# Grouped-query attention: two context tiles of a head pair as one unit of two banks

## What is computed

```python
def mixer_a(u, uc, q_g, k_g, ang, need_ctx):      # 16 query heads of 64, 4 key heads
    ...                                           # normed, rotated q, k, v; qc, kc, vc of the context
    o = gqa_attention(q, jnp.concatenate([kc, k], axis=1),
                      jnp.concatenate([vc, v], axis=1)).reshape(b, s, MIX_WIDTH)
    oc = gqa_attention(qc, kc, vc).reshape(b, n_ctx, MIX_WIDTH) if need_ctx else None
    return o, oc

def gqa_attention(q, k, v):
    scale = HEAD_DIM ** -0.5
    def block(j, qb):
        logits = jnp.einsum("bqhgd,bkhd->bhgqk", qb, k).astype(jnp.float32) * scale
        p = jax.nn.softmax(logits, axis=-1).astype(v.dtype)
        return jnp.einsum("bhgqk,bkhd->bqhgd", p, v)
    return map_query_blocks(block, q)
# afterwards, for both streams: (o * silu(z)) @ w_out, gated, added to the stream
```

## Time and profile before

| | |
|---|---|
| median of 3 runs | 2858.49 us |
| lowest and highest run | 2858.04 and 2862.38 us |
| span of the profiled execution | 2854.9 us |
| PE busy in the span | 2731.4 us (96%) |
| DVE, ACT, POOL busy | 1577.6, 960.5, 759.7 us |
| layer 0, main units: one unit | 4.42 us |
| layer 0, context units: a group of two | 5.51 us |

### The profile page before, as it was taken

The page is one execution under the profiler, slowest core; times in us unless marked ns, Lnnn a source line. Parts: engine busy times, 40 slices in busy tenths (PEclk is TensorE's granted clock), DMA queues, the critical chain, the costliest instruction groups (busy, mean ns, idle before and its releaser), DMA issues. The chain is left out here.

```text
span 2854.9 us, 57245 instructions
## 1 busy us (share of the span) xinstructions
PE 2731.4 (96%) x23728; PEld 2055.4 (72%) x23728; DVE 1577.6 (55%) x2898; ACT 960.5 (34%) x2229; POOL 759.7 (27%) x957
## 2 busy tenths in 40 slices
PE   7999999999999999989999999999999898999999
PEld 4978788785746888744688867547888576458884
DVE  4666776864437746522653267239833774276662
ACT  2022323324422236632121158221212774122660
POOL 3322323220024500012322125136531322244000
PEclk8999999999999999999999999999999999999999
DMA  6230100102431121112111162021111311212100
GB/s 236 91 126 20 43 18 3 49 35 89 159 114 37 60 104 60 61 59 103 37 54 59 60 218 57 37 96 59 48 45 56 133 61 59 74 65 89 75 2 30
DMA packets 108419, 205.86 MB, mean 72 GB/s; under 512 B 21923, under 2 KB 26162, under 8 KB 107648
## 3 DMA queue, kind: packets, MB, share of 16 engines
q1 hardware_dynamic: 107888, 201.30, 20.1%
q0 software_dynamic: 272, 0.89, 0.1%
HBM read 186.85 MB, written 15.54 MB: 71 GB/s over the span
## 5 line engine op out<-in xcount | busy, mean ns | idle before, releaser
L726 PE MATMUL psum<-weights,h_t 128*128 128x256 f32 x1488 | 353.8, 381 | 5.5 <-ACT early_work L815 5.5
L726 PEld LDWEIGHTS psum<-weights,h_t 128*128 128x128 f32 x1488 | 279.7, 190 | 45.2 <-ACT early_work L815 6.7
L2021 PE MATMUL psum<-weights,q_l 128*128 128x512 f32 x576 | 249.7, 592 | 0.0
L1411 DVE TENSOR_REDUCE neg_max<-psum 128x1 f32<-128x768 f32 (+1 forms) x192 | 164.5, 863 | 73.1 <-PE psum L1282 52.9
L2021 PEld LDWEIGHTS psum<-weights,q_l 128*128 128x128 f32 x576 | 108.3, 190 | 130.6 <-issue 130.6
L726 PE MATMUL psum<-z_l,x_tiles 128*128 128x256 f32 x816 | 192.8, 379 | 0.5 <-POOL z_l L941 0.5
L826 ACT ACTIVATE early_work<-psum 128x512 f32<-128x512 f32 (+1 forms) x80 | 45.0, 566 | 377.0 <-DVE psum L1099 247.8
L726 PEld LDWEIGHTS psum<-z_l,x_tiles 128*128 128x128 f32 x816 | 155.0, 190 | 22.0 <-issue 0.9
L1375 ACT ACTIVATE prob<-psum,neg_max 128x768 f32<-128x768 f32 (+1 forms) x160 | 130.8, 819 | 13.7 <-DVE neg_max L1411 9.5
L1463 POOL TENSOR_TENSOR z_l<-z_l,inv_total 128x128 f32<-128x128 f32 x80 | 32.0, 400 | 385.2 <-DVE inv_total L1422 329.6
L2122 DVE TENSOR_TENSOR delta<-psum,gate 128x512 f32<-128x512 f32 x44 | 30.4, 691 | 175.9 <-PE psum L2021 175.9
(11 more groups left out here) (448 smaller groups left out, 6068.6 us busy)
## 6 DMA issues: line engine op xcount, KB each, us to landing
weights<-in_ada_w_dram SPq DMA_DIRECT2D x30, 2048.0 KB, 8.0
weights<-in_a_w_in_dram SPq DMA_DIRECT2D x10, 2048.0 KB, 7.9
weights<-in_b_w_in_dram SPq DMA_DIRECT2D x8, 2048.0 KB, 7.9
weights<-in_c_w_in_dram SPq DMA_DIRECT2D x8, 2048.0 KB, 7.9
weights<-in_w_in_dram SPq DMA_DIRECT2D x6, 2048.0 KB, 7.7
x_aside<-x_tiles SPq DMA_DIRECT2D x24, 512.0 KB, 2.6
x_tiles<-x_aside SPq DMA_DIRECT2D x4, 3072.0 KB, 15.4
weights<-in_a_w_out_dram SPq DMA_DIRECT2D x4, 2048.0 KB, 7.9
```

The costliest lines, as they stand in the source:

```text
L726: last = pe.matmul(dst, lhs[:, k, :], rhs[k // 2][:, k % 2, :], start=k == 0, stop=k == KH - 1)
L1411: last = dve.tensor_reduce(neg_max[:, i % 4, m:m + 1], score(i, m, 0, keys), AX, ALU.max, negate=True)
L2021: last = pe.matmul(pr.bank(4 + u % 4), m_t[:, k, P * t:P * t + P], w[:, k, :], start=(k == 0), stop=(k == KT - 1))
```

## The change

The two context tiles of a head pair become one unit (`joined`), so layer 0 has 32 main units and 8 joined units instead of 48. Per joined unit: four score matmuls of 256 columns, tile beside tile in one bank per head, in a place of two banks; three such places hold three units. The maxima are two reductions, one for each head over both tiles. The exponentials stay four, of 256 columns. The turned blocks of a head go into the bank that held its scores; ACT takes that of head 0, DVE that of head 1. The mix is four matmuls of 256 columns instead of eight of 128. The outputs (256 columns) and the turned gate (256 columns) of a unit share a bank, 6 and 7 in turn, and `gate_t` is used by halves. The gate's copy on ACT stands behind the exponentials of the step and waits for the mix. The gate of the last main group moves the same way into bank 6. The modulation's six row sums and their columns are now spread over the main units alone: ahead of scores 6, 11, 15, 20, 24 and 28, and the columns in step 27 instead of 41. For layer 3 and for the latent attention the lists of instructions are the same as before.

```diff
@@ pair_units
-        for u, tile in enumerate(pair["tiles"]):
-            units.append(dict(group=len(groups), col=u, last=u == len(pair["tiles"]) - 1, **tile))
+        if pair.get("joined"):
+            units.append(dict(group=len(groups), col=0, last=True, joined=True, tiles=pair["tiles"]))
+        else:
...
@@ pair_attention
+    single = sum(not u["joined"] for u in units)
-        at = (c + 1) * n // 7
+        at = (c + 1) * single // 7
...
+    late_gates = {i + 1: u["group"] for i, u in enumerate(units) if u["last"] and single < n and i >= single - 1}
...
+    def joined_bank(i, m):
+        return pr.bank(2 * ((2 * single - 3 + i - single) % 3) + m)
+    def late_bank(i, gate):
+        if i == single - 1:
+            return TURN if gate else OUT
+        return pr.bank(6 + (i - single) % 2)[:, CTX * gate:CTX * gate + CTX]
...
@@ tensor
+        def joined_score(i):
+            if i == single + 1:
+                pe.wait_ge(*exped.at(2 * single - 1))
+            else:
+                before = single - 2 if i == single else single - 1 if i == single + 2 else i - 3
+                for g in range(2):
+                    pe.wait_ge(*taken(before, g))
+            for t, tile in enumerate(units[i]["tiles"]):
+                for m in range(2):
+                    last = pe.matmul(joined_bank(i, m)[:, CTX * t:CTX * t + CTX], tile["q"][m], tile["k"][m],
+                                     start=True, stop=True)
+                    if t:
+                        last.then_inc(*scored.tick())
...
+        def joined_turn(i):
+            for m in range(2):
+                pe.wait_ge(*exped.at(2 * i + m + 1))
+                for x in range(4):
...
+        def joined_mix(i):
+            for m in range(2):
+                pe.wait_ge(*taken(i, m))
+            for kt in range(2):
+                for m in range(2):
+                    weights = prob_t[:, i % 2, 4 * m + 2 * kt:4 * m + 2 * kt + 2, :].rearrange("p x q -> p (x q)")
+                    last = pe.matmul(late_bank(i, 0)[64 * m:64 * m + 64, :], units[i]["tiles"][0]["v"][m][kt], weights,
+                                     start=(kt == 0), stop=(kt == 1))
...
@@ the loop of tensor
             if 0 <= i < n:
                 do_turn(i)
+            if i in late_gates:
+                late_gate(i)
             if i >= 1:
                 do_mix(i - 1)
@@ scalar
+        def late_gate(i):
+            group = late_gates[i]
+            act.wait_ge(*mixed.at(i))
+            act.wait_ge(*finished.at(group if i <= single + 1 else group - 1))
+            act.activation(late_gate_t(i - 1), late_bank(i - 1, 1), ACT.Copy).then_inc(*gate_out.tick())
...
@@ the loop of scalar
-            take_turned(i, 0)
+            if not joined(i):
+                take_turned(i, 0)
             if i + 1 < n:
                 do_exp(i + 1, 0)
+            if joined(i):
+                take_turned(i, 0)
...
             if i + 1 < n:
                 do_exp(i + 1, 1)
+            if i in late_gates:
+                late_gate(i)
@@ vector, do_max
+            if joined(i):
+                dve.tensor_reduce(neg_max[:, i % 4, 2 * m:2 * m + 2],
+                                  joined_bank(i, m).rearrange("p (t k) -> p t k", t=2), AX, ALU.max, negate=True)\
...
@@ vector, finish
+            if groups[group]["last"] + 1 in late_gates:
+                i = groups[group]["last"]
+                dve.wait_ge(*gate_out.at(group + 1))
+                dve.tensor_tensor(groups[group]["dst"], late_bank(i, 0), late_gate_t(i), ALU.mult).then_inc(*finished.tick())
+                return
```

More of the change, by code:

```diff
@@ L1170, in pair_units @@
     for pair in pairs:
-        for u, tile in enumerate(pair["tiles"]):
-            units.append(dict(group=len(groups), col=u, last=u == len(pair["tiles"]) - 1, **tile))
+        if pair.get("joined"):
+            units.append(dict(group=len(groups), col=0, last=True, joined=True, tiles=pair["tiles"]))
+        else:
+            for u, tile in enumerate(pair["tiles"]):
+                units.append(dict(group=len(groups), col=u, last=u == len(pair["tiles"]) - 1, joined=False, **tile))
         groups.append(dict(dst=pair["dst"], last=len(units) - 1, z=[t["z"] for t in pair["tiles"]]))
@@ L1195, in pair_attention @@
     for c in range(6 if next_mod else 0):
-        at = (c + 1) * n // 7
+        at = (c + 1) * single // 7
         mod_rows_at[at - 1 if units[at]["last"] else at] = c
-    gates_at = {i + 2: u["group"] for i, u in enumerate(units) if u["last"]}
+    late_gates = {i + 1: u["group"] for i, u in enumerate(units) if u["last"] and single < n and i >= single - 1}
+    gates_at = {i + 2: u["group"] for i, u in enumerate(units) if u["last"] and i + 1 not in late_gates}
     rows_at = {i + 2: c for i, c in mod_rows_at.items()}
@@ L1201, in pair_attention, with joined @@
     mod_cols_at = max(mod_rows_at, default=-4) + 1
+    def joined(i):
+        return i < n and units[i]["joined"]
     def kts(i):
-        return units[i]["keys"] // P
+        return 4 if joined(i) else units[i]["keys"] // P
     def parts(i):
@@ L1319, in do_mix @@
             last.then_inc(*mixed.tick())
+        def late_gate(i):
+            group = late_gates[i]
+            pe.wait_ge(*scaled.at(i))
+            if i == single:
+                pe.wait_ge(*taken(*in_turn[-1]))
+            elif i == single + 1:
+                pe.wait_ge(*gate_out.at(group))
+            else:
+                pe.wait_ge(*finished.at(group - 1))
+            for x, z in enumerate(groups[group]["z"]):
+                pe.transpose(late_bank(i - 1, 1)[:, P * x:P * x + P], z, pr.eye[:, :])
         def turn_gate(i):
@@ L1368, in do_exp @@
         def do_exp(i, m):
+            if joined(i):
+                joined_exp(i, m)
+                return
             keys = units[i]["keys"]
@@ L1421, in do_inverse @@
                 dve.wait_ge(*scaled.at(i - 3))
-            dve.reciprocal(inv[:, i % 4, :], total[:, i % 4, :]).then_inc(*summed.tick())
+            sums = slice(0, 4 if joined(i) else 2)
+            dve.reciprocal(inv[:, i % 4, sums], total[:, i % 4, sums]).then_inc(*summed.tick())
         def take_turned(i, g):
@@ L1445, in vector @@
                 do_max(i + 1, 0)
-            if i < n and parts(i) > 1:
+            if i < n and parts(i) > 1 and not joined(i):
                 take_turned(i, 1)
@@ L1449, in vector @@
                 do_max(i + 1, 1)
+            if joined(i):
+                take_turned(i, 1)
             if i == 0 and beside_second:
@@ L3611, in grouped_pairs @@
                           z=z_s[:, t, P * j:P * j + P]) for t in queries]
[L3612 removed]
+            pairs.append(dict(tiles=tiles, dst=q_t[:, j, P * queries[0]:P * (queries[-1] + 1)], joined=queries[0] >= XT))
     return pairs
```

56 lines of the change are left out of this document (49 added, 7 removed).

## The result

| set | after, median (lowest to highest) | before, median | ratio, 95% interval |
|---|---|---|---|
| first | 2845.94 (2844.69 to 2850.15) | 2858.88 | 0.9949, 0.9938 to 0.9961 |
| second | 2848.13 (2846.05 to 2855.38) | 2860.73 | 0.9959, 0.9947 to 0.9972 |
| third | 2850.67 (2849.13 to 2854.05) | 2860.97 | 0.9970, 0.9958 to 0.9982 |

The change makes the kernel faster. The ratios put the gain at 8.6 to 14.6 us in the three sets; their mean, 0.9959, is 11.6 us. The medians of each set differ by 12.9, 12.6 and 10.3 us. The profiled executions differ by the same 11.6 us: 2854.9 before, 2843.3 after. The forecast was 10.2 us.

What follows compares the result with a forecast made beforehand. A ring of waits, with no engine full, was taken to bound the context groups. The stretch's -15.3 and the main units' +5.1 gave -10.2 us, from 2858.5 to 2848.3 us; range 2845.0 to 2855.0 us.

Steps and rivals of the forecast that it cites:

- a ring through the gate's copy and the finish: Joined units: gate's copy, finish, reciprocal, maxima, exponentials and ACT's copy wait on each other in turn, 4.0 us per unit.
- Rival B: Joined units: the ring does not close, PE's 3.43 us per unit rules; 2845.5 us in all; 12%.
- C: Rival, joined units: ACT and DVE steps cost more (reduction 0.95, exponentials 0.56 to 0.66 apart); 2850.7 to 2854.5 us; 15%.
- D: Rival, joined units: two heads' matmuls no longer side by side, scores and mix 1.9 each; 2858 us, no change; 6%.
- PE per joined unit: PE's work for scores, turned blocks, gate and mix of one joined unit: 3.43 us, against 3.94 per old group.
- lead-in: From the turned blocks of unit 30 to those of unit 33: 12.1 us without a wait, before it was 10.7.
- six distances: Six joined units after the lead-in: two at 3.4, one 3.8, two 4.0, last 3.7; 22.3 us.
- end: From the last joined unit's turned blocks to the end of the last finish: 5.7 us.
- surcharge for hand-overs: Added behind the lead-in because the same walk over old groups gave 5.31 where the trace has 5.51: 0.7 us.
- stretch: Rebuilt part, turned blocks of unit 30 to the last finish's end: 40.8 us, 15.3 less than 56.1.
- main part: Main units of layer 0 take in two row sums (3.7 us), the columns (0.9) and a wait (0.5): 5.1 us longer.
- the columns' wait: Step 27 of the main units: PE waits for DVE to add the last rows behind score 28, 0.5 us.

Runs made afterwards that it cites:

- The experiments on the finish: Against the changed kernel: DVE's finish one step later, 2847.44 us, again 2845.5; one added reduction ahead of each joined finish, 2852.65; two, one execution, 2857.89.

## Why the prediction came out as it did

**The bound was named rightly.** A ring of waits, not a full engine, set the pace before; this is read from the waits of its trace, and no run tested it by itself. In the joined units a ring through the gate's copy and the finish took its place: 3.91 against the forecast 4.0, from the fourth distance on (the third is 3.86 against 3.8). The experiments on the finish (3.32 without it, 4.26 and 4.59 with more of it) show this directly. Rival B's pace, that of PE (3.43 forecast, 3.32 measured), rules once the finish is out of the ring; it didn't rule in the changed kernel. C did not occur: a reduction lasts 0.66 to 0.69, not 0.95, and the exponentials start 0.45 to 0.47 apart. D did not either: score and mix cost 1.06 and 1.02, not 1.9 each.

**The terms.**

| term | forecast | measured |
|---|---|---|
| PE per joined unit | 3.43 | 3.32 |
| ring | 4.0 | 3.91 |
| lead-in | 12.1 | 11.95 |
| six distances | 22.3 | 21.87 |
| end | 5.7 | 5.62 |
| surcharge for hand-overs | 0.7 | the parts came out 0.66 below their 40.1 |
| stretch | 40.8 | 39.44 |
| main part | +5.1 | +4.92 |

**Mis-sized: the surcharge.** The step "it leaves small hand-overs out; scaled over the part behind the lead-in I add 0.7" failed. The walk over the old groups (5.31, for which the prediction shows no working) was 0.20 short, and I carried that over to the new ones. Scaled as the sentence says, it would even be 1.1 (0.20 of 5.31, over 28.0 us), so the 0.7 was also reckoned wrongly, and by chance the forecast lay 0.4 nearer for it. The new walk had its errors upward without any surcharge: 0.15, 0.43 and 0.08 us in the three parts. So it needed none. This is half of the 1.4 us by which the stretch was overestimated; the other half is those three errors.

**Mis-sized: PE per unit.** Turned blocks and gate cost 0.93 + 0.31 = 1.24, not 1.02 + 0.34. They are ten transposes of one shape in a row, and a unit has three changes of shape: score, transposes, mix. On the line through four transposes (0.59) and twelve (1.46) ten are 1.24. I had given the gate a fixed part of its own. The Trainium skill says in TensorEngine Tiling (Array Packing), Tiling Modes, Key Properties, that changing the tiling mode drains the engine, not going to another tile of the same mode. The trace agrees, by the 1.24.

**Mis-sized: the columns' wait.** 0.24 instead of 0.5, in the changed kernel and in the kernel before with the sums moved. The two row sums were right, 1.87 against 1.86, and the weights caused no wait.

**From 10.2 to 11.6.** Stretch and main part give -16.69 + 4.92 = -11.8 instead of -15.3 + 5.1, and the next stage's first matmul comes as much earlier, at 1238.11 instead of 1249.87. In the whole span 11.6 are left. Seven eighths of what the forecast missed is the stretch's 1.4.

**The range failed in one step**: "with 0.5 us for the spread of the runs". Its lower end allowed a gain of 13.5 us. The mechanism gave 11.6, well inside, but the first ratio says 14.6, with an interval of 11.1 to 17.7, and the later ones 11.7 and 8.6. Of the 4.4 us between the forecast 10.2 and this 14.6 the terms above explain 1.4; the other 3.0 no trace here shows as an effect of the change. A spread of 3 us around the mechanism belonged in the range. It could have been seen: three runs of the kernel before spread over 4.3 us.

**The offset was wrong too.** "The median lies 3.6 above the span" was true of the three runs, and was carried over to the changed kernel. But in all traces here an execution's own time lies 1.7 to 1.9 above its span (2845.16 with 2843.3, 2846.05 with 2844.2, 2841.89 with 2840.1). By that the profiled execution of the kernel before took about 2856.7 us, and the other 1.8 us of the 3.6 were scatter. The first set of after has its median 2.6 above the span, and the forecast time was 1.0 too long for that. A trace says what a part costs, and not where the median of the runs will lie.

## What to carry to other kernels

When a buffer that limits the work in flight is widened, write down the next ring of waits before pricing the change, with each instruction on its engine's own list; here it ran through a finish that the data did not need so early. Late, unurgent steps (a finish, a gate's copy) go behind the work that feeds the next exponential: moving one call took 3.35 us more off a stretch of 39. Then ask again whether the extra buffer pays: the third place was worth nothing before that edit and 1.5 us after it. This gain is read from the traces; the timed ratios can't part the two kernels.

## What the hardware showed unexpectedly

**A group's start on PE belongs to the change of shape, not to the group or its passes.** Turned blocks and gate, two groups with a wait in the list between them, cost together what one group of ten transposes would by the rows of before: 1.24. Sixteen passes of 128 columns lasted 1.09, eight of 256 lasted 1.08.

**One reduction that gives two results costs no more than its columns.** A reduction of 128x512 to two maxima was 0.69 ahead of the exponential that needs it, and two of them took 1.26, while two of 256 columns to one maximum took 0.76 together and one of 768 columns took 0.95.

**The clock at a slack end.** PE busy for 4.09 of 5.51 us and for 3.54 of 3.91 kept 1.00. With one reduction more in the finish it fell to 0.51 for 3.4 us at the end of the stage, behind 2.69 busy of 4.4; with two, to 0.50 at the start of the next stage. The Trainium skill tells in TensorE: Matmul & The Clock Gate, HAM oscillation — how this bites in real kernels, of a kernel in which waits for DMA let the clock fall so that the next burst starts slow. Here PE's waits in the units were for ACT's exponentials (and once, with two reductions more, for POOL), not for DMA, and the second fall cost 1.4 us (5.18 instead of 3.81). What made the clock fall in these two executions and not in the others was not tested. No joined unit of the changed kernel was hit.

**The same kernel, another arrival.** Layer 0 began between 1049.0 and 1063.7 us in the traces of this study, with the granted clock between 300 and 500 us at 1.00 to 0.97, though not in step: at 0.98 the changed kernel arrived once at 1049.9 and once at 1056.8. From its first turned blocks to the last finish its three executions are alike to 0.05 us. Most of the scatter between executions comes from outside the part under study; why the clock differs wasn't found.
